# Modulation vectors by chunks of four column groups, and the first attention's wide bias by TensorE

## What is computed

```python
# first attention, per block of 128 queries
sc = jnp.einsum('bqhcd,bkhcd->bhcqk', q_blk, k).astype(f32) * scale
bias = jnp.take(rel_table, bucket, axis=0).astype(f32)      # per head, shared by both c
sc = jnp.where(causal_mask(i, s), sc + bias, NEG_INF)
a = jax.nn.softmax(sc, axis=-1)
wts = a[:, :, 0] - lam * a[:, :, 1]

# second block, per layer i: d = 1024, w_mod[i] is 1024 x 3072
silu_c = jax.nn.silu(c)
silu_cc = jax.nn.silu(c_ctx)
mod_x = (silu_c @ w_mod[i] + b_mod[i])[:, None, :]
mod_c = silu_cc @ w_mod[i] + b_mod[i]
sh_x, sc_x, g_x = jnp.split(mod_x, 3, axis=-1)
sh_c, sc_c, g_c = jnp.split(mod_c, 3, axis=-1)
hx = rms_norm_2(x, norm_g[i]) * (1.0 + sc_x) + sh_x
```

## Time and profile before

| | us |
|---|---|
| median of 3 runs (1326.38 to 1327.38) | 1327.18 |
| span of the profiled execution, first to last instruction | 1325.0 |
| TensorE matmul busy | 1271.4 (96%) |
| VectorE busy | 945.7 (71%) |
| ScalarE busy | 723.9 (55%) |
| GpSimd busy | 391.0 (30%) |
| share of TensorE in the chain that ended last | 78% |

### The profile page before, as it was taken

The page is one execution under the profiler, slowest core; times in us unless marked ns, Lnnn a source line. Parts: engine busy times, 40 slices in busy tenths (PEclk is TensorE's granted clock), DMA queues, the critical chain, the costliest instruction groups (busy, mean ns, idle before and its releaser), DMA issues.

```text
span 1325.0 us, 24391 instructions
## 1 busy us (share of the span) xinstructions
PE 1271.4 (96%) x8908; PEld 1102.8 (83%) x8908; DVE 945.7 (71%) x1426; ACT 723.9 (55%) x1257; POOL 391.0 (30%) x377
## 2 busy tenths in 40 slices
PE   5999999999999999999999999999989999999996
PEld 4887899999999877898999998888855699987666
DVE  6878588888878985558988887853377548454674
ACT  5555455655567777545565657644366515413562
POOL 4942144545431140143445452011012320000022
PEclk9999999999999999999999999999999999999999
DMA  8565246666645542155576663322200274522100
GB/s 309 178 218 191 72 141 233 219 222 219 217 154 172 160 130 96 63 191 171 197 234 211 230 213 128 130 93 95 96 1 1 59 181 133 170 95 80 48 1 32
DMA packets 52665, 191.72 MB, mean 145 GB/s; under 512 B 6048, under 2 KB 6304, under 8 KB 52320
## 3 DMA queue, kind: packets, MB, share of 16 engines
q1 hardware_dynamic: 43488, 158.59, 36.2%
q0 software_dynamic: 8368, 31.33, 7.5%
q10 hardware_dynamic: 720, 0.57, 0.2%
HBM read 189.41 MB, written 1.05 MB: 144 GB/s over the span
## 4 chain that ended last, share of the span: by engine, by line
PE 78%; DVE 9%; ACT 7%; issue 3%; POOL 1%; DMA 1%; SPq 0%; DVEq 0%; ACTq 0%; POOLq 0%
PE G L417 13%; PE G L419 13%; PE G L418 13%; PE A L417 6%; PE A L419 6%; PE A L418 6%; DVE WL L1131 3%; PE R L651 3%; PE R L578 2%; PE R L558 2%; ACT WH L1848 2%; PE A L999 1%; PE R L417 1%; PE R L419 1%; PE R L418 1%
## 5 line engine op out<-in xcount | busy, mean ns | idle before, releaser
L1131 DVE TENSOR_TENSOR WL<-RAW,WH 128x1024 fp32r<-128x1024 f32 x295 | 390.4, 1330 | 245.3 <-ACT WH L1848 244.9
L1848 ACT ACTIVATE WH<-RAW 128x1024 fp32r<-128x1024 f32 x295 | 310.4, 1057 | 387.1 <-PE G L419 275.9
L417 PE MATMUL G<-XH,WH 128*128 128x256 f32 (+1 forms) x1336 | 398.7, 298 | 7.8 <-DVE WL L1131 4.6
L419 PE MATMUL G<-XH,WL 128*128 128x256 f32 (+1 forms) x1336 | 395.4, 296 | 0.0
L418 PE MATMUL G<-XL,WH 128*128 128x256 f32 (+1 forms) x1336 | 395.4, 296 | 0.0
L417 PEld LDWEIGHTS G<-XH,WH 128*128 128x128 f32 x1336 | 255.5, 191 | 21.6 <-issue 10.6
L418 PEld LDWEIGHTS G<-XL,WH 128*128 128x128 f32 x1336 | 255.6, 191 | 7.4
L419 PEld LDWEIGHTS G<-XH,WL 128*128 128x128 f32 x1336 | 255.7, 191 | 6.2
L417 PE MATMUL A<-HH,WH 128*128 128x256 f32 x352 | 99.9, 284 | 1.0 <-POOL HL L2477 1.0
L418 PE MATMUL A<-HL,WH 128*128 128x256 f32 x352 | 99.8, 283 | 0.0
L419 PE MATMUL A<-HH,WL 128*128 128x256 f32 x352 | 99.7, 283 | 0.0
(11 more groups left out here) (355 smaller groups left out, 2532.0 us busy)
## 6 DMA issues: line engine op xcount, KB each, us to landing
RAW<-in_wst SPq DMA_DIRECT2D x295, 512.0 KB, 4.1
M<-in_wmod POOLq DMA_DIRECT2D x48, 512.0 KB, 4.1
B<-in_rpb POOLq DMA_DIRECT2D x4, 1024.0 KB, 12.6
H<-in_x_t SPq DMA_DIRECT2D x2, 512.0 KB, 8.4
M<-in_x_tok SPq DMA_DIRECT2D x1, 1024.0 KB, 13.5
M<-in_ctx_t POOLq DMA_DIRECT2D x1, 1024.0 KB, 5.2
out_y<-M SPq DMA_DIRECT2D x2, 384.0 KB, 2.7
C<-in_cst SPq DMA_DIRECT2D x1, 737.0 KB, 15.1
```

Source lines behind the costliest of these rows:

```text
L417: mm(out, lh, rh, start=start, stop=False, skip_group_check=True)
L419: return mm(out, ll, rh, start=False, stop=stop, skip_group_check=True)
L1131: v.tensor_tensor(WL[:, slot, :], RAW[:, raw, :], WH[:, slot, :].bitcast(F32), ALU.subtract).then_inc(w_lo, 1)
L1848: act(WH[:, slot, :], RAW[:, raw, :], ACT.Copy).then_inc(w_hi, 1)
```

## The change

`w_mod` is laid out anew: 24 chunks of 1024 KB, each one block of 128 rows k against 2048 columns; eight chunks make a third. `modulate` takes a chunk with four f32 matmuls of 512 columns: the stationary operand is the same vector block each time, and matmul g writes rows 32 g to 32 g + 31 of the bank `O`, a column group of its own. The first eight chunks are taken before and inside the first attention (two ahead of it, then one at every second step from n = 2 to 12), and none behind it. The others are taken in the feed-forward parts, eight each, at tiles 6, 8, 10 and so on to 20, now in f32 too: no rounding on ScalarE, no subtraction on VectorE; GpSimd copies the vector block to `SV` ahead of each load there. `RM` has three buffers of 1024 KB (two of them in use in the feed-forward parts). The turn behind each third is four transposes. The bias of units with two key tiles is added by TensorE: two more f32 matmuls, identity times `TB`, into the scores' banks. Units with one key tile keep the addition on VectorE.

```diff
-RMS = 6
-MODS = 48
-PLAIN = 16
+RMS = 3
+CHUNKS = 8
...
+            def modulate(vectors, buf, start, stop):
+
+                for g in range(4):
+                    m = mm(O[32 * g:32 * g + 32, :], vectors, RM[:, buf, g, :], start=start, stop=stop, skip_group_check=True)
+                m.then_inc(m_used, 1)
+
             def fill(n):
 
                 for _ in range(n):
-                    i, k = divmod(fills[0], KD)
-                    if fills[0] == 0:
+                    k = fills[0]
+                    if k == 0:
                         pe.wait_ge(m_sil, 1)
-                    if k == 0:
-                        pe.wait_ge(m_raw[i % RMS], 16 * (i // RMS + 1))
-                    g, q = i // 4, i % 4
-                    out = O
-                    m = mm(out[32 * g:32 * g + 32, q * P:(q + 1) * P], SC[:, k, :], RM[:, i % RMS, k * P:(k + 1) * P],
-                           start=(k == 0), stop=(k == KD - 1), skip_group_check=True)
-                    if k == KD - 1:
-                        m.then_inc(m_used, 1)
+                    pe.wait_ge(m_raw[k % RMS], 16 * (k // RMS + 1))
+                    modulate(SC[:, k, :], k % RMS, k == 0, k == CHUNKS - 1)
                     fills[0] += 1
...
-                    if n < len(units) + 2:
-                        fill(filler)
+                    if n in filler:
+                        fill(1)
...
                     m = mm(out[c][:, 0:nk * P], QT[64 * c:64 * c + 64, h, qt * P:(qt + 1) * P],
-                           KT0[64 * c:64 * c + 64, h, 0:nk * P], start=True, stop=True, skip_group_check=True)
+                           KT0[64 * c:64 * c + 64, h, 0:nk * P], start=True, stop=qt == 0, skip_group_check=True)
+                if qt:
+                    for c in range(2):
+                        m = mm(out[c][:, 0:nk * P], IDT, TB[:, h, P:P + nk * P], start=False, stop=True, skip_group_check=True)
...
-            fill(12)
+            fill(2)
             pe.wait_ge(bias_ok, 1)
-            attention("l0", scores_l0, value_l0, 5)
-            fill(14)
+            attention("l0", scores_l0, value_l0, range(2, 14, 2))
             heads_turn(0)
-            fill(6)
             heads_turn(1)
-            fill(6)
...
+                def modulated(buf, turn, start=False, stop=False):
+
+                    pe.wait_ge(r_vec[buf], turn + (v0 + 1))
+                    pe.wait_ge(r_raw[buf], turn * 16 + 16 * (v0 + 1))
+                    modulate(SV[:, buf, :], buf, start, stop)
+
                 for j in range(2, 7):
                     tile(j)
+                modulated(0, 0, start=True)
                 with pe.Fori(0, 3) as i:
-                    for d in range(4):
-                        tile(7 + d, i, d)
-                for d in range(3):
-                    tile(19 + d)
-                    refill(layer, d, 3)
+                    tile(7, i)
+                    tile(8, i)
+                    modulated(1, i)
+                    tile(9, i)
+                    tile(10, i)
+                    modulated(0, i + 1)
+                tile(19)
+                tile(20)
+                modulated(1, 3, stop=True)
+                tile(21)
                 down(0, p0 + 64, hb + FT - 1, p0 + 64, False, False)
-                refill(layer, 3, 3)
                 down(1, p0 + 65, hb + FT, p0 + 65, False, True)
...
-                k0 = 0 if qt == 0 else P
-                return v.tensor_tensor(sc, sc, bc(TB[:, h, k0:k0 + nk * P], 2), ALU.add)
+                return None if qt else v.tensor_tensor(sc, sc, bc(TB[:, h, 0:P], 2), ALU.add)
...
+            def chunks(first, end):
+
+                for k in range(first, end):
+                    if k >= RMS:
+                        gp.wait_ge(m_used, k - RMS + 1)
+                    gp.dma_start(RM[:, k % RMS, :, :].rearrange("p g c -> p (g c)"), wmod[k]).then_inc(m_raw[k % RMS], 16)
...
+                    gp.wait_ge(m_used, i * 2 + (first + k - 1))
+                vectors = SC[:, k, :] if k < 2 else SC[:, bass.ds(i * 2 + k, 1), :].rearrange("p a c -> p (a c)")
+                g.tensor_copy(SV[:, k % 2, :], vectors).then_inc(r_vec[k % 2], 1)
+                src = wmod[first + k] if k < 2 else wmod[bass.ds(i * 2 + (first + k), 1)].rearrange("a p c -> p (a c)")
+                gp.dma_start(RM[:, k % 2, :, :].rearrange("p g c -> p (g c)"), src).then_inc(r_raw[k % 2], 16)
...
             gp.wait_ge(t_mm, 1)
-            panels(0, 2)
+            chunks(0, 1)
             gp.wait_ge(t_mm, 2)
-            panels(2, 4)
+            chunks(1, 2)
             gp.wait_ge(bias_ok, 1)
+            chunks(2, 5)
...
             for h in range(8):
-                upto = min(PLAIN, 6 + (10 * h + 35) // 8)
-                panels(nextp, upto)
-                nextp = upto
+                if 1 <= h < 4:
+                    chunks(4 + h, 5 + h)
                 head_squares(h)
```

More of the change, by code:

```diff
@@ L330, in program @@
         sum_step = sem("sum_step")
-        r_raw = [sem(f"r_raw{i}") for i in range(4)]
-        r_hi, r_lo, r_y = sem("r_hi"), sem("r_lo"), sem("r_y")
+        r_raw = [sem(f"r_raw{i}") for i in range(2)]
+        r_vec = [sem(f"r_vec{i}") for i in range(2)]
         h_sq = sem("h_sq")
@@ L623, in advance, with attention @@
                     next(unit, None)
-            def attention(s, scores, value, filler=0, behind=None, meanwhile=(0, 0), first=0, last=None, ready=()):
+            def attention(s, scores, value, filler=(), behind=None, meanwhile=(0, 0), first=0, last=None, ready=()):
                 units = attn_units(s)
@@ L852, in ple @@
                         row_parts(b, False)
[L853 removed]
+                        turn_modulators(O, 2 + layer)
             ffn(0)
@@ L909, in _ @@
                                 + [(1, k) for k in range(8, 16)], T, lambda k: pe.wait_ge(at_g, AJ0["l1"] + k // 2 + 1))
-            attention("l1", scores_l1, value_l1, 0, first_o, (4, 3), first=2, ready=((1, TVALS),))
+            attention("l1", scores_l1, value_l1, (), first_o, (4, 3), first=2, ready=((1, TVALS),))
             advance(first_o, 32)
@@ L1025, in _ @@
             evacuated(pe, U0["a_z"] + 7)
-            attention("a", scores_a, value_a, 0, first_o, (2, 2), first=4)
+            attention("a", scores_a, value_a, (), first_o, (2, 2), first=4)
             advance(first_o, KD)
@@ L1099, in _ @@
             first_o = head_unit("b_o", [(c, k) for c in range(2) for k in range(7)] + [(0, 7), (1, 7)], T, lambda k: pe.wait_ge(at_o, AT_JOBS["a"] + k + 1))
-            attention("b", scores_b, value_b, 0, first_o, (6, 3), first=2, ready=((0, TVALS + 10), (1, TVALS + 12)))
+            attention("b", scores_b, value_b, (), first_o, (6, 3), first=2, ready=((0, TVALS + 10), (1, TVALS + 12)))
             advance(first_o, 2 * KD)
@@ L1397, in with_bias @@
             def with_bias(layer, r, t0, rows):
-                n = rows.shape[-1] if len(rows.shape) == 2 else rows.shape[-1] * rows.shape[-2]
+                n = rows.shape[-1] * rows.shape[-2]
                 at = VC[f"bm{layer}"] + t0
-                dst, bias = MD[:, layer, r, t0:t0 + n], V[:, at:at + n]
-                if len(rows.shape) == 3:
-                    dst, bias = (x.rearrange("p (g q) -> p g q", q=4) for x in (dst, bias))
+                dst, bias = (x.rearrange("p (g q) -> p g q", q=4) for x in (MD[:, layer, r, t0:t0 + n], V[:, at:at + n]))
                 link(v.tensor_tensor(dst, rows, bias, ALU.add))
@@ L2487, in ffn @@
                         hidden(d % 2, i * 4 + (hb + 6 + d), i * 12 + (p0 + 3 * d + 19))
-                        gathers(layer, 2 + d, i)
+                        if d % 2:
+                            gathers(layer, 2 + d // 2, i)
                 for j in range(18, FT):
                     hidden(j % 2, hb + j, p0 + 3 * j + 1)
-                    if j < 20:
-                        gathers(layer, j - 4, 0)
-            def panels(first, end):
-                for i in range(first, end):
-                    if i >= RMS:
-                        gp.wait_ge(m_used, i - RMS + 1)
-                    gp.dma_start(RM[:, i % RMS, :], wmod[i]).then_inc(m_raw[i % RMS], 16)
@@ new lines, in gathers @@
+            def gathers(layer, k, i):
+                first = CHUNKS * (layer + 1)
+                if k < 2:
+                    gp.wait_ge(m_used, first)
+                else:
+                    gp.wait_ge(m_used, i * 2 + (first + k - 1))
[3 more added lines that the diff above has]
+                gp.dma_start(RM[:, k % 2, :, :].rearrange("p g c -> p (g c)"), src).then_inc(r_raw[k % 2], 16)
```

101 lines of the change are left out of this document (21 added, 80 removed).

## The result

The changed kernel takes **1330.51 us** (median of 7 runs, 1328.40 to 1332.18) against 1327.18 (7 runs, 1326.05 to 1328.14): ratio **1.0028**, interval 1.0018 to 1.0039. It is slower, by 3.3 us in the medians and 3.7 by the ratio; 1320.1 was forecast. The profiled execution spans 1328.2 us against 1325.0.

What follows compares the result with a forecast made beforehand. TensorE was taken as full in the feed-forward loops and first attention, VectorE close behind there, with latency chains at the ends. Terms -9.8 + 5.3 - 2.6 = -7.1 gave 1320.1 us; range 1312.5 to 1331.

Steps and rivals of the forecast that it cites:

- the price of a chunk in the attention: Four f32 matmuls of 512 columns in four column groups take 1.0 us on TensorE, between 0.86 and 3.42.
- two groups at a time: Rival: TensorE streams only two moving operands at once, so a chunk takes 1.88 us; 1337.7 us in all, chance 0.12.
- turns: Rival: a chunk's four matmuls run one after another, 3.42 us a chunk; 1368.5 us in all, chance 0.04.
- estimate by its share of the ideal: Chunk price by the skill page's 2.38 times for three column tiles: 1.08 us, making the sum 1.6 us longer.
- where TensorE waits, and how long: First attention: TensorE waits for late loads at chunks 2, 5 and 7, for 4.3, 3.2 and 3.2 us.
- the rival of the clock: Rival: TensorE's clock falls to half pace after each of three load waits; 1324.6 us in all, chance 0.12.
- With a fall at each, 4.5 us: Clock rival's cost for pauses of 4.3, 3.2 and 3.2 us, from 1.5 us lost by TensorE's first eight matmuls.
- the pause in these rows was over twice as long as any of the three: Argument against the clock rival: the half-pace first matmuls followed 11.1 us of standing; forecast pauses were 4.3, 3.2, 3.2.
- 5.3 us lost: Inside the first attention: the last unit's maximum starts at 139.4 against 134.14, with waits at chunks 2, 5 and 7.
- 2.6 us gained: From the last value matmul to the first projection: without 26 fills, VectorE's path ends at 146.8 instead of 149.42.
- Gain 4.9 us each: Two feed-forward parts: 14 refills of 0.92 us saved, 12.9, eight chunks added, 8.0; 9.8 us together.
- the latency to the last remainder: After each feed-forward part's last hidden tile: the last product still waits 8.44 us, leaving TensorE idle some 2.7 us.

Runs made afterwards that it cites:

- the kernel busy behind the units: Changed kernel with chunks 5 to 7 requested one head earlier, chunks 2 to 7 multiplied two units later, eight unread products around the turns of heads: 1317.26 us.
- the fastest kernel: Changed kernel with earlier requests, attention chunks in iterations 6, 8, 10 and 17 and two behind the units, last feed-forward chunk before the last product: 1307.90 us.
- the last kernel of the table: The kernel of 1307.90 us with the bias of units with two key tiles added by VectorE again: 1311.47 us.

## Why the prediction was wrong

The step that failed is that all work behind a pause was priced at full clock. Between the forecast (-7.1) and the span (+3.2) lie 10.3 us, and 6.8 of them follow the clock: 4.3 inside the attention (2.7 behind the first pause, 1.6 behind the third), 1.0 in the first projection and 1.5 behind d0. The rest is 1.6 us of small terms inside the attention, 1.5 in the feed-forward parts, 0.1 behind the units and 0.3 behind d1. The time lies within the range (1312.5 to 1331) only because the range reached over the rivals; the forecast itself was on the other side of no change.

**Right: the price of a chunk in the attention** (1.0; measured 0.99), which had carried most of the doubt. The rivals of two groups at a time and of turns are off: four groups run 3.6 times as fast as one behind the other (3.55 / 0.99). The Trainium skill (TensorE: Matmul & The Clock Gate, Measured speedup vs the span model) gives 2.38 times for three column tiles. My estimate by its share of the ideal was 1.08 us; this chunk, with 0.99, does not agree.

**Right: where TensorE waits, and how long.** Forecast 4.3, 3.2 and 3.2 us at chunks 2, 5 and 7, measured 4.94, 2.86 and 3.07: 10.87 against 10.7.

**Wrong: the rival of the clock, in its price and its chance.** "With a fall at each, 4.5 us" priced 1.5 us a fall, from the eight first matmuls; "the pause in these rows was over twice as long as any of the three" was taken against it, and it got 0.12. The row only showed that 11 us of standing ends at half pace; it said nothing of 3 us. It had to be read as one bound, not as a threshold. It also showed a pace and no granted clock: the windows view of the kernel before gives 1.00 for 11 to 15 us, though the matmuls start 0.43 us apart there. The fall behind the first pause alone cost 2.7 us, since not eight matmuls but all until 112.7 ran at half pace. I also counted too few pauses: at the three waits I looked, at the pauses of 2.46 and 1.99 us behind the last units and of 1.85 before the last product I did not, though the change itself makes them, by taking out the fills of the last steps, the 26 behind them and the last refill. The Trainium skill (TensorE: Matmul & The Clock Gate, Part 1) says that an idle window returns the array to half rate; behind the first wait the rows of the changed kernel agree, at 1.94 us for a chunk against 0.99, but not behind the wait of 2.86 us, with 1.06.

**Wrong in size: "5.3 us lost" inside the attention.** The maximum of the last unit starts at 145.33, not 139.4: 11.2 lost. The waits were right in their sum, so the other 5.9 are mostly pace: with TensorE kept busy in the same waits p - a is 3.5 us shorter, though chunk 2 landed 0.8 us later after the first scores there. The remaining 1.6 (5.9 - 3.5 - 0.8) are small terms: 0.2 is the later a and 0.2 the longer waits; 0.4 lie before chunk 2, which TensorE reached at 101.82 and so 2.8 us behind a instead of 2.4, and 0.5 between chunk 7 and the last maximum at full clock (7.42 instead of 6.87); 0.3 lie in the pairs between. At both places ScalarE stands on TensorE's way (a wait of 0.34 us at 101.33, a copy of 0.39 us in the chain at 141.91), which the counting left out.

**Right in the sum: "2.6 us gained" after the attention** (2.5: 145.33 to 158.10 is 12.77, and 134.14 to 149.42 was 15.28). The parts listed there add up to 4.56 us and not 4.7, which is what was measured (153.41 to 158.10). That full clock would have gained more is not shown: where the second turn of the heads ran at full pace (1.26 us instead of 1.97, chunks asked for earlier), TensorE then waited 0.76 us for VectorE's remainders, and from the last transposes to the projection it was 8.31 us instead of 8.39. A term that was missing is 1.0 us in the first projection, which starts at half pace: f - p is 30.45 against 29.49.

**Wrong in size: "Gain 4.9 us each".** Measured 4.18 and 4.10, from two errors of opposite sign. The chunk costs 1.2 us in the loop, not 1.0, so the loop gains 12.9 - 8 x 1.2 = 3.3. TensorE's timeline of the changed kernel:

```profile
259.77 0.28 PE L413 MATMUL A<-HH,WL 128*128 128x256 f32 x1
259.98 1.06 PE L545 MATMUL R<-M,SV 128*32 128x512 f32 x8
260.98 0.38 PE L411 MATMUL G<-XH,WH 128*128 128x256 f32 x1
261.20 0.28 PE L412 MATMUL G<-XL,WH 128*128 128x256 f32 x1
```

The matmuls of the loop start 0.12 apart; before the chunk it is 0.21, and behind its first successor 0.22. All eight chunks of layer 0 have these edges. The refills were of the loop's own type and had none, and neither has a chunk between the f32 matmuls of the attention (four starts of scores in 0.42 us before it, 0.99 to the next start). And the latency to the last remainder, taken as fixed at 8.44 us, is 7.42 (377.79 to 385.21): GpSimd's operation before it takes 0.73 instead of 1.73 us, for a reason that no run shows. So the idle stretch is 1.85, not 2.7, and 1.0 us more is gained. Moving the last chunk there gained 1.17 us, which is the chunk at its full price.

**Missing: 1.5 us between d0 and ffn1**, the clock behind the pause at 385.36.

The terms again: forecast -9.8 + 5.3 - 2.6 = -7.1; measured -8.3 (feed-forward) + 11.2 - 2.5 + 1.0 (projection) + 1.5 (behind d0) + 0.3 (behind d1) = +3.2, the span. The price of the parts of the change was nearly right; at what pace TensorE works after it has waited was left out of it.

## What to carry to other kernels

Fills in a latency chain look free to remove, and are not: before taking them out, list every pause that this opens, and price the work behind each at half clock until a row shows otherwise. When one larger transfer takes the place of several, look at what stands between it and its request on the issuing queue; here one line's move brought 8.4 us. What measures as nothing in one state of a kernel (the bias on TensorE) can be worth some 3.7 us once the wait that hides it is gone, so try it again in the mended kernel.

## What the runs showed of the hardware that was not expected

- **Four column groups of 32 in f32, 512 columns**: 0.99 us at once, 3.55 in turn.
- **The clock falls behind short pauses, but not behind each.** In the changed kernel it fell in or right behind pauses of 4.94, 3.07 and 2.46 us, and not at the one of 2.86 us in the same execution. At the pause of 1.99 us it was at half already; with chunks asked for earlier it had come back to 1.00 by then and fell behind that pause too. The pause of 1.85 us before the last product of layer 0 was followed by half pace in the changed kernel (first fence), the one of 1.92 in layer 1, with the same code around it, by full pace (1.00 from 802 to 810 us), and so was one of 1.87 with chunks in the feed-forward parts only (second fence):

```profile
385.95 0.41 PE L411 MATMUL A<-HH,WH 128*128 128x256 f32 x1
386.17 0.41 PE L412 MATMUL A<-HL,WH 128*128 128x256 f32 x1
```

```profile
376.50 0.28 PE L413 MATMUL A<-HH,WH 128*128 128x256 f32 x1
376.62 0.28 PE L414 MATMUL A<-HL,WH 128*128 128x256 f32 x1
```

  Whether a pause near 2 us costs anything thus differs even within one execution; no run here settles what decides. It may also spread the times, though four runs of each are few: four runs of the kernel busy behind the units went from 1315.3 to 1321.6 us, four of the fastest kernel, which has no such pause in the attention, from 1307.7 to 1309.5.
- **Several short pauses do it too**: in the last kernel of the table the clock fell at 126 us, and since 110 us it had had no pause but waits of 0.3 to 0.9 us for VectorE.
- **A change between f32 and the loop's matmul type costs 0.09 us before and 0.10 behind**, at each chunk of the feed-forward loop (starts 0.21 and 0.22 us apart instead of 0.12).
